# A two-layer decoder trunk in split float32: when tables are loaded, one split moved ahead of a weight sum, and the closing norm rearranged

## The reference

```python
def rms_norm(x, g):
    y = x * lax.rsqrt(jnp.mean(x * x, axis=-1, keepdims=True) + 1e-6)
    return y * g

def swiglu_ffn(h, w_up, w_down):            # w_up 1024 x 5632, w_down 2816 x 1024
    gate, up = jnp.split(h @ w_up, 2, axis=-1)
    return (jax.nn.silu(gate) * up) @ w_down

for l in range(2):
    x = x + 0.5 * swiglu_ffn(rms_norm(x, norm_ffn1[l]), ffn1_up[l], ffn1_down[l])
    h = rms_norm(x, norm_mix[l])
    x_pool, q_lat, kv_lat, k_rope, gate_logits = jnp.split(h @ w_in[l], SPLIT_POINTS, axis=-1)
    gates = jax.nn.sigmoid(gate_logits + b_gate[l])
    # branch_a: causal pooling of x_pool; branch_b: attention on q_lat, kv_lat (each
    # normalised with q_latent_norm, kv_latent_norm) and k_rope
    x = x + (gates[0] * branch_a + gates[1] * branch_b) @ w_out[l]
    x = x + 0.5 * swiglu_ffn(rms_norm(x, norm_ffn2[l]), ffn2_up[l], ffn2_down[l])
return rms_norm(x, final_norm)
```

## Time and profile before

| | |
|---|---|
| median of 3 runs | 1105.1 us (1101.61 to 1105.96) |
| profiled execution | 1105.38 us, its span 1103.6 us (1.8 us lie around the span) |
| granted TensorE clock, mean | 0.998 |
| busy: PE, DVE, ACT, POOL | 1088.1, 884.1, 646.5, 77.3 us |
| `w_up` loads | 172 of 512 KB, median 4.9 us from issue to landing |
| `w_down` loads | 44 of 1024 KB, median 4.8 us |
| `b_gate` loads | 4 of 1024 KB, median 8.0 us |

### The profile page before, as it was taken

One profiled execution on the slowest core, in us unless ns is written; L12 is line 12 of the kernel. 1 busy time (PEld: TensorE's weight loads), 2 busy tenths in 40 slices (PEclk: granted clock), 3 DMA queues, 4 the chain that ended last, 5 costly groups with the idle time before them and its releaser, 6 DMA issues.

```text
span 1103.6 us, 15444 instructions
## 1 busy us (share of the span) xinstructions
PE 1088.1 (99%) x5341; PEld 911.9 (83%) x5341; DVE 884.1 (80%) x1144; ACT 646.5 (59%) x819; POOL 77.3 (7%) x97
## 2 busy tenths in 40 slices
PE   9999899999999999999999999999999999999997
PEld 6788688988988888888888888888899888888886
DVE  4989788766776689888879888976668776988896
ACT  5656465555963466656556656645568436665663
POOL 0029100100110000000010000001002000000001
PEclk9999999999999999999999999999999999999999
DMA  8566764653644555556576556547445355655641
GB/s 266 194 214 212 268 196 163 214 179 120 206 154 153 182 181 193 187 190 218 178 254 230 179 191 223 173 140 273 146 127 200 134 178 171 205 176 191 222 172 61
DMA packets 140187, 207.31 MB, mean 188 GB/s; under 512 B 5208, under 2 KB 103712, under 8 KB 139632
## 3 DMA queue, kind: packets, MB, share of 16 engines
q1 hardware_dynamic: 137616, 197.16, 53.9%
q0 software_dynamic: 2096, 8.99, 2.4%
q10 hardware_dynamic: 432, 0.59, 0.2%
HBM read 205.66 MB, written 1.05 MB: 187 GB/s over the span
## 4 chain that ended last, share of the span: by engine, by line
PE 92%; DVE 3%; DMA 2%; ACT 2%; issue 1%; POOL 0%; POOLq 0%; ACTq 0%; SPq 0%; DVEq 0%
PE psum L1618 29%; PE psum L1620 29%; PE psum L1619 29%; DMA raw<-ffn_down_dram 2%; PE psum L1709 2%; PE psum L1636 2%; DVE w_lo L1050 1%; ACT w_hi L676 0%; PE psum L1911 0%; DVE xs L1050 0%; DMA ident<-c_ident_dram 0%; ACT scores L867 0%; PE psum L1700 0%; ACT xs L855 0%; PE psum L1944 0%
## 5 line engine op out<-in xcount | busy, mean ns | idle before, releaser
L1050 DVE TENSOR_TENSOR w_lo<-raw,w_hi 128x1024 fp32r<-128x1024 f32 (+6 forms) x276 | 414.2, 1526 | 86.7 <-ACT w_hi L676 81.6
L1618 PE MATMUL psum<-w_hi,xT 128*128 128x512 f32 (+2 forms) x984 | 383.7, 390 | 2.0 <-DVE w_lo L1050 1.8
L1620 PE MATMUL psum<-w_hi,xT 128*128 128x512 f32 (+2 forms) x984 | 380.0, 386 | 0.0
L1619 PE MATMUL psum<-w_lo,xT 128*128 128x512 f32 (+2 forms) x984 | 379.5, 386 | 0.0
L676 ACT ACTIVATE w_hi<-raw 128x2048 fp32r<-128x2048 f32 (+4 forms) x168 | 286.4, 1711 | 74.4 <-PE psum L1620 69.0
L1618 PEld LDWEIGHTS psum<-w_hi,xT 128*128 128x128 f32 x984 | 185.2, 188 | 42.0 <-DVE w_lo L1050 3.2
L1620 PEld LDWEIGHTS psum<-w_hi,xT 128*128 128x128 f32 x984 | 185.1, 188 | 37.2
L1619 PEld LDWEIGHTS psum<-w_lo,xT 128*128 128x128 f32 x984 | 185.2, 188 | 34.6 <-issue 0.2
L793 ACT ACTIVATE oT<-xs 128x1024 fp32r<-128x1024 f32 x72 | 76.4, 1062 | 69.6 <-DVE xs L1050 69.6
L761 ACT ACTIVATE scores<-psum,stat 128x256 f32<-128x256 f32 x88 | 41.2, 472 | 112.1 <-PE psum L1620 111.1
L1050 DVE TENSOR_TENSOR oT<-xs,oT 128x1024 fp32r<-128x1024 f32 x72 | 88.1, 1228 | 0.0
(11 more groups left out here) (221 smaller groups left out, 1418.6 us busy)
## 6 DMA issues: line engine op xcount, KB each, us to landing
raw<-ffn_up_dram SPq DMA_DIRECT2D x172, 512.0 KB, 4.9
raw<-ffn_down_dram SPq DMA_DIRECT2D x44, 1024.0 KB, 4.8
raw<-w_in_dram SPq DMA_DIRECT2D x20, 1024.0 KB, 5.1
raw<-w_attn_proj_dram SPq DMA_DIRECT2D x8, 1024.0 KB, 4.9
raw<-w_out_dram SPq DMA_DIRECT2D x8, 1024.0 KB, 4.9
raw<-w_uq_dram SPq DMA_DIRECT2D x8, 576.0 KB, 4.1
gates<-b_gate_dram POOLq DMA_DIRECT2D x4, 1024.0 KB, 8.0
raw<-w_ukv_dram SPq DMA_DIRECT2D x8, 512.0 KB, 3.9
```

The source lines that it names most:

```text
L1050: return dve.tensor_tensor(dst, a, b, ALU.subtract)
L1618: nc.tensor.matmul(dst, a_hi, b_hi, start=first, stop=False)
L1619: nc.tensor.matmul(dst, a_hi, b_lo, start=False, stop=False)
L1620: return nc.tensor.matmul(dst, a_lo, b_hi, start=False, stop=last)
```

## The change

Four edits. (1) In `rest(L)`, in both layers, the two bias loads wait for the seventh and the eighth `plainB_hi` of that layer's first FFN, and the latent gains (and with them the gain of the next norm) for the ninth; before, nothing held them. (2) In layer 0's first FFN alone, DVE's split of the second chunk's slot 0 stands ahead of `addB_first` instead of behind it. (3) At the end ACT squares x/32, so that DVE need only add the two halves' sums and the epsilon, with the first half's part taken as soon as it is there. (4) At the end each row block's half 0 is multiplied by the gain on POOL, ahead of the root, and scaled by ACT; half 1 is DVE's. The store of (t 1, h 0) is issued by ACT, the other three by SP.

The diff, without the new constant, the moved `out_v` and the changed parameter of `rsqrt`:

```diff
@@ -505,11 +508,9 @@
                 ffn(L, 1)
 
 
-            out_v = out.rearrange("b (t p) d -> p (b t) d", p=P)
-            for t in range(TB):
-                for h in range(2):
-                    sp.wait_ge(out_rows[h], t + 1)
-                    sp.dma_start(out_v[:, t, half(h)], xs[:, t, half(h)]).then_inc(out_landed, 16)
+            for t, h in ((0, 0), (0, 1), (1, 1)):
+                sp.wait_ge(out_rows[h], t + 1)
+                sp.dma_start(out_v[:, t, half(h)], xs[:, t, half(h)]).then_inc(out_landed, 16)
             sp.wait_ge(out_landed, 16 * TB * 2)
 
 
@@ -617,17 +618,19 @@
             pool.wait_ge(exponent_set, 2)
             def rest(L):
 
+                for t in range(TB):
+                    pool.wait_ge(plainB_hi.sem, plainB_hi.upto(L, SEVEN - TB + t))
+                    broadcast(gates[:, t, :], b_gate[bass.ds(L, 1), :], bias_landed)
+                pool.wait_ge(plainB_hi.sem, plainB_hi.upto(L, SEVEN))
                 broadcast(lat_gain[:, 0:QR], q_latent_norm[bass.ds(L, 1), :], latg_landed)
                 broadcast(lat_gain[:, QR:QR + KVR], kv_latent_norm[bass.ds(L, 1), :], latg_landed)
-                for t in range(TB):
-                    broadcast(gates[:, t, :], b_gate[bass.ds(L, 1), :], bias_landed)
                 next_gain(L, 0)
                 next_gain(L, 1)
                 norm_rsqrt(L, 1)
                 for i in range(2):
                     pool.wait_ge(lat_ms.sem, lat_ms.upto(L, i + 1))
                     rs = stat[:, LRS + 2 * i:LRS + 2 * i + 2]
-                    rsqrt(rs, stat[:, LMS + 2 * i:LMS + 2 * i + 2], 2, lat_rstd)
+                    rsqrt(rs, stat[:, LMS + 2 * i:LMS + 2 * i + 2], 2, lat_rstd.sem)
 
                     pool.wait_ge(lat_rstd.sem, lat_rstd.upto(L, i + 1))
                     pool.tensor_tensor(rs, rs, stat[:, NRS:NRS + TB], ALU.mult).then_inc(lat_scale.sem, 1)
@@ -642,13 +645,11 @@
             def last_rows():
 
                 for t in range(TB):
+                    pool.wait_ge(final_x, 2 * t + 1)
+                    pool.tensor_tensor(xs[:, t, half(0)], x[:, t, half(0)], gain[:, half(0)],
+                                       ALU.mult).then_inc(final_gained, 1)
                     pool.wait_ge(final_ms, t + 1)
-                    pool.tensor_tensor(stat[:, NRS + t:NRS + t + 1], stat[:, NMS + t:NMS + t + 1], half_neg[:, 0:1],
-                                       ALU.pow).then_inc(final_rstd, 1)
-                    if t == 0:
-                        pool.wait_ge(final_x, 3)
-                        pool.tensor_tensor(xs[:, 1, half(0)], x[:, 1, half(0)], gain[:, half(0)],
-                                           ALU.mult).then_inc(final_gained, 1)
+                    rsqrt(stat[:, NRS + t:NRS + t + 1], stat[:, NMS + t:NMS + t + 1], 1, final_rstd)
 
 
             norm_rsqrt(0, 0)
@@ -1031,11 +1032,13 @@
                     act.wait_ge(final_x, 2 * t + h + 1)
                     if t or h:
                         act.wait_ge(final_sq, 2 * t + h)
-                    act.activation(square_junk[:, half(h)], x[:, t, half(h)], ACT.Square,
+                    act.activation(square_junk[:, half(h)], x[:, t, half(h)], ACT.Square, scale=1.0 / ROOT_D,
                                    accum_out=stat[:, LSQ + 2 * t + h:LSQ + 2 * t + h + 1]).then_inc(final_sq, 1)
-            act.wait_ge(final_rstd, TB)
-            act.wait_ge(final_gained, 1)
-            act.activation(xs[:, 1, half(0)], xs[:, 1, half(0)], ACT.Copy, scale=rstd(1)).then_inc(out_rows[0], 1)
+                act.wait_ge(final_rstd, t + 1)
+                act.wait_ge(final_gained, t + 1)
+                act.activation(xs[:, t, half(0)], xs[:, t, half(0)], ACT.Copy, scale=rstd(t)).then_inc(out_rows[0], 1)
+            act.wait_ge(out_rows[0], TB)
+            act.dma_start(out_v[:, 1, half(0)], xs[:, 1, half(0)]).then_inc(out_landed, 16)
 
 
         @block.vector
@@ -1197,23 +1200,22 @@
                         mul_add(x[:, t, half(h)], psum[:, 2 * t + h, :], 0.5, x[:, t, half(h)]).then_inc(final_x, 1)
                     if t == 0:
                         final_mean(0)
-                final_scale(0, 0)
+                final_scale(0)
                 final_mean(1)
-                final_scale(0, 1)
-                final_scale(1, 1)
+                final_scale(1)
 
             def final_mean(t):
-                part, ms = stat[:, LMS + t:LMS + t + 1], stat[:, NMS + t:NMS + t + 1]
+                c, part = LSQ + 2 * t, stat[:, LMS + t:LMS + t + 1]
+                dve.wait_ge(final_sq, 2 * t + 1)
+                dve.tensor_scalar(part, stat[:, c:c + 1], EPS, None, ALU.add).then_inc(final_part, 1)
                 dve.wait_ge(final_sq, 2 * t + 2)
-                dve.tensor_scalar(part, stat[:, LSQ + 2 * t:LSQ + 2 * t + 1], 1.0 / D, EPS,
-                                  ALU.mult, ALU.add).then_inc(final_part, 1)
                 dve.wait_ge(final_part, t + 1)
-                mul_add(ms, stat[:, LSQ + 2 * t + 1:LSQ + 2 * t + 2], 1.0 / D, part).then_inc(final_ms, 1)
-
-            def final_scale(t, h):
+                dve.tensor_tensor(stat[:, NMS + t:NMS + t + 1], stat[:, c + 1:c + 2], part, ALU.add).then_inc(final_ms, 1)
+
+            def final_scale(t):
                 dve.wait_ge(final_rstd, t + 1)
-                dve.scalar_tensor_tensor(out=xs[:, t, half(h)], in0=x[:, t, half(h)], scalar=rstd(t),
-                                         in1=gain[:, half(h)], op0=ALU.mult, op1=ALU.mult).then_inc(out_rows[h], 1)
+                dve.scalar_tensor_tensor(out=xs[:, t, half(1)], in0=x[:, t, half(1)], scalar=rstd(t),
+                                         in1=gain[:, half(1)], op0=ALU.mult, op1=ALU.mult).then_inc(out_rows[1], 1)
 
             def into_ffn2(L):
 
@@ -1340,8 +1342,12 @@
             def ffn(L, f):
                 q0 = f * FFN2_0 // RING
                 hidden_product(L, f, 0)
-                addB_first(L, f, 0)
-                split(L, q0 + 1, 0)
+                if f == 0 and L == 0:
+                    split(L, q0 + 1, 0)
+                    addB_first(L, f, 0)
+                else:
+                    addB_first(L, f, 0)
+                    split(L, q0 + 1, 0)
                 plainB(L, f, 0)
                 addA(L, f, 0)
                 plainA(L, f, 0)
```

More of the change, by code:

```diff
@@ L43 @@
 EPS = 1e-6
+ROOT_D = 32.0
+assert ROOT_D * ROOT_D == D
 THETA = 10000.0
@@ L307, in trunk @@
         ups, downs = (ffn1_up, ffn2_up), (ffn1_down, ffn2_down)
+        out_v = out.rearrange("b (t p) d -> p (b t) d", p=P)
         def blk(t):
@@ L540, in rsqrt @@
             def rsqrt(dst, src, width, done):
-                return pool.tensor_tensor(dst, src, half_neg[:, 0:width], ALU.pow).then_inc(done.sem, 1)
+                return pool.tensor_tensor(dst, src, half_neg[:, 0:width], ALU.pow).then_inc(done, 1)
             def norm_rsqrt(L, s):
@@ L546, in norm_rsqrt @@
                     pool.wait_ge(ms_done.sem, ms_done.upto(L, TB * s + t + 1))
-                    rsqrt(stat[:, NRS + t:NRS + t + 1], stat[:, NMS + t:NMS + t + 1], 1, rstd_done)
+                    rsqrt(stat[:, NRS + t:NRS + t + 1], stat[:, NMS + t:NMS + t + 1], 1, rstd_done.sem)
             step = [0]
```

## The result

| | before | after |
|---|---|---|
| median of 8 runs each | 1102.9 us (1100.69 to 1105.96) | 1097.16 us (1096.46 to 1099.59) |
| ratio, 95% interval | | 0.994 (0.9927 to 0.9953) |
| profiled execution, its span | 1105.38, 1103.6 us | 1096.62, 1094.8 us |
| PE busy | 1088.1 us | 1085.1 us |

The kernel became 0.6% faster; 1097.9 was forecast. By the ratio this is 6.6 us, and the interval stands for 5.2 to 8.1 us; the two medians are 5.7 us apart.

A forecast was written before the change was run, and what follows sets the result against it. PE was taken as the bound, busy 1088.1 of 1103.6 us, leaving only gaps, lower clock, head and tail. -5.40 - 1.35 - 0.75 = -7.5 us against 1105.38 gave 1097.9 us, range 1095.5 to 1102.5.

The forecast's parts named there:

- Edit 1, -5.4: Two loop passes from 104.41 us: moving the tables removes the late w_down tile's 5.40 us loss, idle PE plus clock.
- the new places: Three passes of each layer's first FFN: tables cost nothing, about 0.1 MB left at w_down issue; up to 2.7 us each.
- slot 0 w_up loads: Loads issued at 107.98 and rounded at 118.93: in more danger from the tables, with 10.95 us of slack at ACT.
- The slack of 8.4 us: Loop w_down tiles: PE waits only once a tile takes over 8.4 us to land.
- Edit 2, -1.35: Layer 0's first FFN, second chunk: with the split first PE's 1.42 us gap goes, gaining 1.35 us; bounds 0 and 1.83.
- Edits 3 and 4, -0.75: Kernel's end: squares, last root and stores together gain 0.75 us; bounds +0.5 and -1.1.
- the late squares: Kernel's end: ACT's last squaring starts 0.25 us late, behind a scaling now ahead of row block 1's squares.
- the root: Kernel's end: no DVE scaling left beside the last root, so 0.55 us instead of 0.99, a gain of 0.45.
- the store by ACT: Kernel's end: ACT issues one of the last two stores beside SP's, saving one issue, about 0.4 us.
- The little collision: Rival: tables still collide a little at six places, 0.3 to 0.9 us each, say 1101.5 us; chance 0.17.
- the six stalls: Rival: w_down shares with a table at six passes, up to 2.7 us each, 1114 us; chance 0.05.
- The third rival: Stall was this run's: edit 1 brings about 2 us, about 1101; chance 0.13, shared with an end without gain.

The follow-up runs named there:

- e6: Changed kernel with its tables in the same passes and portions, but issued at the same moment as the w_down load: 1097.23 us, ratio 0.9937.
- e9: Changed kernel with both bias loads (2 MB) issued right behind the seventh pass's w_down load: 1097.12 us, ratio 0.9933 to the kernel before.
- e11: Changed kernel with ACT's squares ahead of its scaling of block 0, all stores by SP and POOL's window copy held: 1097.23 us, ratio 0.9935.
- e1: Kernel before with the tables held back alone: 1098.35 us against 1103.98, ratio 0.9952.
- e4: Kernel before, unchanged, run and profiled once more: 1104.94 us, ratio 1.0006.
- e12: As e9, but the two bias loads wait for the seventh pass's first weight sum, so are issued ahead of the w_down load: 1098.35 us, ratio 0.9956.
- e5: Changed kernel with all 2.8 MB of a layer's tables issued at the seventh `plainB_hi`: 1099.62 us, ratio 0.9954 to the kernel before.
- e7: Changed kernel with all four stores issued by SP, as before: 1097.26 us, ratio 0.9932 to the kernel before.
- e10: Changed kernel with POOL's window-table copy held until the sums of the sixth pass are made: 1097.9 us, ratio 0.9936 to the kernel before.

## Why the prediction was right

The forecast was -7.5 us; the runs show -6.6 by the ratio (5.2 to 8.1). That the absolute time, 1097.16, came within 0.8 us of the 1097.9 forecast is in part luck: it was reckoned from 1105.1, the median of three runs of before, and the median of eight is 1102.9. The five variants in which no table costs time (`e6` to `e9`, `e11`) have ratios of 0.993 to 0.9937 against the kernel before, which is 7.0 to 7.7 us and nearer the forecast.

- **Edit 1, -5.4.** Right in place, mechanism and size: `e1` has -5.3. The number came from one stretch of one profile, and the four profiles with the old tables have 5.4 to 7.5, so it was the smallest of them. That it still fits the runs is partly luck: the four profiles have 6.4 us in the mean, the runs of `e1` 5.3, which would follow if some executions have a small stall or none (see `e4`). That layer 1 gains nothing held.
- **Why the new places are free.** They cost nothing, but the reason given was half right. The argument was bytes left in flight, and for 1 MB issued 6.6 us ahead almost nothing is left; that held (5.0 us). What it missed is the order: bytes issued ahead of the tile delay it (9.0 us by 2 MB issued 1.1 ahead in `e12`, 9.5 by 2.8 MB with 6.6 us of lead in `e5`, 11.9 to 12.6 by 2.8 MB with about 2.5), bytes issued behind it far less (4.8 to 6.8 in `e6` and `e9`). The slot 0 w_up loads were rightly held to be the most in danger: the later one took 9.1 us in that pass though the table was issued behind it, under the 10.95 worked out.
- **The slack of 8.4 us** stood the test: 6.8 us cost nothing, 9.0 and 9.5 cost 0.38 and 0.88 us of idle PE in layer 0, some 0.2 less than they exceed it by.
- **Edit 2, -1.35.** Right on PE's way: 0.95 to 1.5 by the profiles. The run times alone leave it open (0.4 faster, between 1.7 faster and 0.8 slower).
- **Edits 3 and 4, -0.75.** The step that was mis-sized: -0.3. Up to the last scaling the forecast was -0.35 (the late squares +0.25, DVE's shorter step -0.18, the root -0.45, rounded) and the profiles have -0.39 (6.59 us from the first of the last updates of x, for 6.98). The term that failed is the store by ACT, priced at -0.4 for an issue saved: from the last scaling to the end it is 3.95 us for 3.86, since both stores then land later (`e7`).
- **The rivals.** The little collision and the six stalls did not come. The third rival, that the stall was this run's, is refuted in its strong form, since the stall came in each of the four profiles. Why one run of before took 1101.61 stays open: the head varies by 2.3 us by itself, and a run with a small stall is not ruled out, since five of 72 later runs were as fast (see `e4`).

## What to carry to other kernels

A bulk transfer that nothing waits for soon can still cost: issue it behind the stream's next urgent load, when that load has nothing in front of it, or so long ahead that it has landed, and look for the moment at which the urgent load is issued, not only at the share of the DMA engines that is busy. Then look at each load near it: one that is the last of several in its queue can still be late. A forecast from one profile pair should say how far the head varies: here 1.75 of 8.8 us between the two spans was none of the change. An issue saved on a second queue is worth nothing until the landing is looked at too.

## What the runs showed of the hardware that was not expected

- Transfers of 0.8 to 2 MB issued by POOL 0.3 us behind a 1 MB load of SP's left it at 4.8 and 4.9 us (4.8 alone), and 0.04 to 0.07 us behind it at 5.8 to 6.8; issued 1.1 us ahead of it they made it 9.0. The bias loads issued behind took 7.0 to 9.4 themselves. That is nearer to service in the order of issue than to even turns. But a 0.5 MB load with three others in front of it on SP's queue took up to 9.1 us, 5.3 to 6.5 without a table, though the table was issued 0.85 us behind it.
- Two stores of 256 KB issued on SP's and ACT's queues at the same moment landed in 2.6 and 2.8 us, one behind the other on SP's in 2.0 and 2.3.
- A POOL copy of 128x1536 beside a DVE instruction with two inputs in the on-chip memory doubled the latter, 1.22 to 2.42 us in `e10`, 1.23 to 2.47 in `e4`. The Trainium skill says that such a DVE instruction contends with a GpSimd instruction that reads the on-chip memory, and that the ports they share are an exclusive lock (SBUF — State Buffer, "Who interferes with whom"). The trace agrees: in `e4` DVE's instruction took longer by 1.24 us, and the copy ran for 1.40 us after DVE's had started. New was that it shows in a pass bound by PE, 0.6 to 0.8 us.
